# A hybrid decoder layer: key and query chunks loaded later, rotated without a wait on the output product, and split behind the weights on ScalarE

## The reference

```python
q = rotary(q); k = rotary(k) * RET_QK ** -0.5
def step(R, chunk):                       # one chunk of 128 tokens, all heads
    inner = (qc @ kc.T * decay_in) @ vc
    cross = (qc @ R) * xi
    R = R * gamma_c + (kc * zeta).T @ vc
    return R, inner + cross
out = (out - mean) * rsqrt(var + EPS) * g_ret     # over each head's 512 values
y_ret = out * silu(gate_ret)
merged = sigmoid(merge_mla) * (y_mla @ w_proj_mla) + sigmoid(merge_ret) * (y_ret @ w_proj_ret)
x = x + gate * (merged @ w_out);  result = rmsnorm(x, g_final)
```

## Time and profile before

| | us |
|---|---|
| median of 3 runs (1618.77, 1622.36, 1622.16) | 1622.16 |
| the profiled execution's own time | 1618.77 |
| its span, first to last instruction | 1617.0 |
| PE busy in it | 1570.6 (97%) |
| DVE busy | 957.6 (59%) |
| ACT busy | 607.2 (38%) |
| POOL busy | 323.1 (20%) |

### The profile page before, as it was taken

One profiled execution on the slowest core, in us unless ns is written; L12 is line 12 of the kernel. 1 busy time (PEld: TensorE's weight loads), 2 busy tenths in 40 slices (PEclk: granted clock), 3 DMA queues, 4 the chain that ended last, 5 costly groups with the idle time before them and its releaser, 6 DMA issues. The chain is left out here.

```text
span 1617.0 us, 20336 instructions
## 1 busy us (share of the span) xinstructions
PE 1570.6 (97%) x7600; PEld 1310.9 (81%) x7600; DVE 957.6 (59%) x1610; ACT 607.2 (38%) x1057; POOL 323.1 (20%) x280
## 2 busy tenths in 40 slices
PE   5999999999999999999999999999999999999998
PEld 4778888888888888788888878887688888888886
DVE  6984444444444457752565665567987775647544
ACT  5444333333333343342343333334544443213111
POOL 2232223322222200200000000016555530000000
PEclk9999999999999999999999999999999999999999
DMA  9132323323223334799254555548977768335432
GB/s 387 37 130 105 111 111 111 111 106 121 112 104 111 98 93 164 311 410 318 80 199 174 168 195 170 179 137 272 308 237 229 247 205 285 112 131 189 143 104 78
DMA packets 142225, 278.70 MB, mean 172 GB/s; under 512 B 11056, under 2 KB 83632, under 8 KB 133552
## 3 DMA queue, kind: packets, MB, share of 16 engines
q1 hardware_dynamic: 125488, 245.09, 43.6%
q10 hardware_dynamic: 12032, 15.54, 2.9%
q0 software_dynamic: 4608, 16.78, 2.6%
HBM read 182.47 MB, written 94.37 MB: 171 GB/s over the span
## 5 line engine op out<-in xcount | busy, mean ns | idle before, releaser
L1567 DVE TENSOR_TENSOR w_form<-w_pair,w_form 128x512 fp32r<-128x512 f32 x150 | 116.3, 776 | 127.3 <-ACT w_form L1202 125.6
L1202 ACT ACTIVATE w_form<-w_pair 128x512 fp32r<-128x512 f32 x150 | 94.6, 632 | 245.3 <-PE p_banks L2072 237.2
L2069 PE MATMUL p_banks<-h_hi,w_form 128*128 128x512 f32 x300 | 116.8, 389 | 1.1 <-DVE w_form L1567 1.1
L2071 PE MATMUL p_banks<-h_lo,w_form 128*128 128x512 f32 x300 | 116.7, 389 | 0.0
L2072 PE MATMUL p_banks<-h_hi,w_form 128*128 128x512 f32 x300 | 116.7, 389 | 0.0
L1271 ACT ACTIVATE prob<-p_banks,neg_max 128x128 f32<-128x128 f32 (+3 forms) x64 | 47.5, 742 | 181.9 <-DVE neg_max L1675 181.9
L524 ACT ACTIVATE w_hi<-w_raw 128x1024 fp32r<-128x1024 f32 (+2 forms) x69 | 59.5, 865 | 142.2 <-PE p_banks L2319 94.4
L2319 PE MATMUL p_banks<-y_hi,w_lo 128*128 128x512 f32 x256 | 99.6, 389 | 0.0
L1046 POOL DMA_DIRECT2D v_ret<-v_stage x32 | 17.4, 544 | 411.5 <-DVE v_stage L1658 411.5
L2318 PE MATMUL p_banks<-y_lo,w_hi 128*128 128x512 f32 x256 | 99.6, 389 | 0.0
L2317 PE MATMUL p_banks<-y_hi,w_hi 128*128 128x512 f32 x256 | 99.6, 389 | 0.0
(11 more groups left out here) (302 smaller groups left out, 4325.0 us busy)
## 6 DMA issues: line engine op xcount, KB each, us to landing
w_pair<-in_w_pairs SPq DMA_DIRECT2D x25, 1024.0 KB, 4.8
w_raw<-in_w_dense SPq DMA_DIRECT2D x45, 512.0 KB, 4.5
v_ret<-v_stage POOLq DMA_DIRECT2D x32, 512.0 KB, 3.4
v_chunk<-v_ret SPq DMA_DIRECT2D x32, 512.0 KB, 3.6
merge_t<-act_t SPq DMA_DIRECT2D x48, 256.0 KB, 3.5
act_t<-stage SPq DMA_DIRECT2D x40, 256.0 KB, 2.0
act_t<-stage_late SPq DMA_DIRECT2D x40, 256.0 KB, 2.0
ada<-in_w_ada SPq DMA_DIRECT2D x4, 2048.0 KB, 23.7
```

The costliest lines, as they stand in the source:

```text
L1202: self.nc.scalar.activation(self.form[f % FORM_SLOTS][:, 0, :], self.form_source(f), ACT.Copy).then_inc(self.form_hi, 1)
L1567: nc.vector.tensor_tensor(self.form[f % FORM_SLOTS][:, 1, :], self.form_source(f), self.form[f % FORM_SLOTS][:, 0, :].bitcast(F32), ALU.su ...
L2069: self.nc.tensor.matmul(out, w_hi[:, cut], x_hi[:, q, :], start=fresh and q == 0, stop=False, skip_group_check=True)
L2071: self.nc.tensor.matmul(out, w_hi[:, cut], x_lo[:, q, :], start=False, stop=False, skip_group_check=True)
```

## The change

Five edits in the retention loop:

1. SP: the load of query and key chunk n + 4 near the end of step n becomes the load of chunk n + 3 at the top of step n. So each of these loads is issued behind the `yr_done` wait, the `y_ret` store and the gate load of the step before, and ahead of the value chunk.
2. POOL: `rotate_chunk` no longer waits for `out_done`.
3. POOL: the scratch tile changes place at chunk 6 and not at chunk 12, and the last stores of value tiles are issued ahead of chunk 6 and not of chunk 9. The wait for all of these stores moves from chunk 12 to chunk 6.
4. ACT: `high_qk(n + 2)` moves from behind `high_chunk(n + 1)` to the end of step n, behind every split of that step. DVE's order stays.
5. DVE: the 128x1 TENSOR_SCALAR of L1781 (times 1.0, times a column) becomes a 128x1 TENSOR_TENSOR.

```diff
@@ sync_attention
             if g == STEPS + 2:
                 self.load_qk_chunk(sp, 2)
-                self.load_qk_chunk(sp, 3)
                 self.load_set0(sp, 1)
@@ sync_retention
             if n + 3 < CHUNK_STEPS:
+                self.load_qk_chunk(sp, n + 3)
                 self.load_v_chunk(sp, n + 3)
...
-            if n + 4 < CHUNK_STEPS:
-                self.load_qk_chunk(sp, n + 4)
             h, m = divmod(n, NT)
             sp.wait_ge(self.yr_done, n + 1)
@@ gpsimd
         for n in range(2, CHUNK_STEPS):
-            if n == 9:
+            if n == 6:
                 for unit in range(units, FILL_UNITS):
                     self.store_fill(pool, unit)
             self.rotate_chunk(pool, n)
@@ rotate_chunk
-        raw, late = self.qk_raw[n % 3], int(n >= 12)
+        raw, late = self.qk_raw[n % 3], int(n >= 6)
...
-        elif n == 12:
+        elif n == 6:
...
-        if n >= 3:
-            pool.wait_ge(self.out_done, n - 2)
@@ scalar_retention
             if n + 1 < CHUNK_STEPS:
                 self.high_chunk(act, n + 1)
-            if n + 2 < CHUNK_STEPS:
-                self.high_qk(act, n + 2)
             if n == len(FILL_LATE) - 1:
...
                 units += 1
+            if n + 2 < CHUNK_STEPS:
+                self.high_qk(act, n + 2)
@@ vector_retention
-            nc.vector.tensor_scalar(self.ret_rstd[:, cell], self.ret_rstd[:, cell], 1.0, t["ret_cols"][:, col:col + 1],
-                                    ALU.mult, ALU.mult).then_inc(self.stats_done, 1)
+            nc.vector.tensor_tensor(self.ret_rstd[:, cell], self.ret_rstd[:, cell], t["ret_cols"][:, col:col + 1],
+                                    ALU.mult).then_inc(self.stats_done, 1)
```

## The result

The changed kernel takes 1650.3 us (median of 4 runs, 1646.9 to 1652.2); the kernel before took 1621.1 us beside it (4 runs). The ratio is 1.018, with a 95% interval of 1.0158 to 1.0201: 1.8% slower. The forecast was 1640 with a range of 1629 to 1651, so direction and range held and the time came out 10 us above the forecast.

What follows compares the result with a forecast made beforehand. PE was taken to bound nearly everywhere, with DVE setting the pace in early steps. Early 13.9 plus later 5.8 us made 19.7, giving 1638.5 from the profiled execution; with the median 3.4 above that, 1640 us, range 1629 to 1651.

Steps and rivals of the forecast that it cites:

- ACT order: Retention loop: DVE waits in `low_qk` for ACT's splits, then does its own late; early steps 8.6 us, later 5.8.
- stores and scratch: Step 4: chunk 6's rotation waits for the value-tile stores to land, holding up ACT's `high_qk(6)`; 2.5 us taken.
- rotation's overlap: Early steps: rotation released by its load runs beside DVE's `low_qk` and splits; net 2.8 us, bounds 0 to 8.
- 128x1 instruction: DVE statistics: new form taken to cost 0 with one element per partition, bounded to 2.6 us either way.
- Order alone: Retention loop: rotations miss DVE's splits, store wait hidden, only the order costs; 8 to 12 us, 1627 to 1634; chance 0.20.
- The clock falls as well: Steps 3 to 6: pauses of 2 us or more bring PE's clock down, adding 6 to 10 us; 1646 to 1655; chance 0.10.
- signs of being wrong: Loop: `out_n` as early as now despite late `low_qk`, clock down for long, or rotations again in DVE's PSUM part.
- Nothing: Early steps: PE's merge and fill matmuls absorb more than seen; total under 5 us, at 1622; chance 0.07.
- faster: Loop: step 5's overlap (1.9 us) and most of the 7.6 us of waits vanish; 1616 at best; chance 0.06.
- eight meetings: First eight steps: DVE instructions each wait for one rotation instruction, up to 1.3 us; up to 8 us, total near 1645.
- The signs named ahead of the result: Profile after: `out_n` waits 10 us or more, `low_qk` behind ACT some 15, new 1 to 2 us waits in steps 15, 22, 29.

Runs made afterwards that it cites:

- the order alone: Kernel before with only ACT's `high_qk` moved behind the splits of its step, DVE's order unchanged; 1637.0 against 1620.4 us, ratio 1.0103.
- order on ACT and DVE: Kernel before with ACT's `high_qk` and DVE's `low_qk` both moved behind the splits of the step; 1627.5 against 1620.4 us, ratio 1.0043.

## Why the prediction was right in direction and short in size

The last column is what the time falls by when the edit is taken out of the changed kernel.

| term, us | forecast | alone | in the changed kernel |
|---|---|---|---|
| ACT order | 14.4 | 16.6 | 17.4 |
| stores and scratch | 2.5 (0.9 to 3.6) | 5.8 | 10.6 |
| rotation's overlap (edits 1, 2) | 2.8 (0 to 8) | 3.4 | -7.6 |
| 128x1 instruction | 0 (-2.6 to 2.6) | 12.4 | 4.8 |
| sum | 19.7 | 38.2 | (29.2 measured) |

- **ACT order: the mechanism right, one part of its path not.** DVE waits in `low_qk` for ACT's splits and is late with its own, as forecast. The early steps cost 10.9 us in the execution that was profiled (8.6 forecast). But PE was to lose them at `out_n`, and with edit 4 alone these waits stay at 4.3 us in steps 2 to 8: PE stops for `y_lo` in step 7 and for the merge addition in step 8 instead. In the later steps, 15 and 16 cost 5.0 together (1.8 forecast), step 22 1.8 and step 29 0.9 (1.4 each); 11, 18 and 25 cost nothing (0.4 each). The pause in step 15 was near in size, +1.7 us in the changed kernel and +2.2 with edit 4 alone against 1.8. The excess is the clock: in the kernel with edit 4 alone PE's busy time grew by 3.7 us in steps 0 to 7 and by 2.8 in steps 15 and 16, and the term had none of it.
- **Stores: the mechanism right, the term mis-sized.** In the changed kernel the last value tile is ready at 1140.43 and ACT comes to `high_qk(6)` 7.2 us later, as forecast. The rotation ends 14.6 us after the tile and not 10.8, so ACT waits 7.5 us and not 3.6, or the 2.5 that I took. The 3.8 us are in the landing: 6.2 us was the median of this stretch before, and here the first of the two stores landed after 7.1 us and the other, which the rotation waits for, after 10.0 (median 8.5):

```profile
v_ret<-v_stage POOLq DMA_DIRECT2D x2, 512.0 KB, 8.5
```

  What makes it longer is edit 4, not edit 1. The five kernels with the early stores fall into two groups:

| kernel | edit 1 | edit 4 | stores issued against the value chunk's load, us | landing, us | DMA engines busy until then |
|---|---|---|---|---|---|
| stores and scratch alone | no | no | 1.2 ahead | 5.4 | 106% |
| changed, without the order | yes | no | 1.2 ahead | 6.3 | 101% |
| changed | yes | yes | 0.2 behind | 8.5 | 99% |
| changed, without the 128x1 instruction | yes | yes | 0.2 behind | 8.7 | 100% |
| changed, without loads and rotation | no | yes | 0.2 behind | 8.2 | 101% |

  The issues in the last of these, which has no edit 1, POOL and SP:

```profile
1139.80 1.19 POOL L1046 DMA_DIRECT2D v_ret<-v_stage  x2 [12.75 <-DVE v_stage L1658]
...
1139.60 0.33 SPq L827 DMA_DIRECT2D v_chunk<-v_ret  x1
```

  With the order changed, `low_qk` of step 3 is late, so the last value tile and its stores are, and they go out together with the next step's loads of a value chunk, a weight and two MLA outputs. The DMA engines are full in all five, so full engines alone do not tell how long a landing takes. That it is the queueing behind those loads which lengthens it is argued and not shown; no run moves the stores alone. The longer wait then joined with the late `y_lo` and the slow clock: 12.5 us of delay in one step.
- **Overlap: near in size alone, in part by luck, and of the wrong sign in company.** 3.4 us against 2.8. Steps 4 and 7 met the rotation as forecast; steps 1 and 2 did not, steps 3 and 6 did, and step 5 gained 0.7 us and not 1.9. That moving the rotation takes away the clash of edit 5 was not in the sum, since I put that edit at zero.
- **The 128x1 instruction: this is the step that failed.** "With one element in each partition I take 0", and a bound of 2.6 us from the 0.29 us of `inner_lo`. The bound came from an instruction that reads PSUM, and the 0 from the instruction's size; alone the edit cost 12.4 us, and 4.8 in company. The row to take was that of the other two-SBUF-input instructions beside a rotation, 0.68 to 1.28 us: what they lose is not a share of their own length but the rest of POOL's instruction, and a tiny instruction loses as much as a large one. That the rotation of before starts when DVE is at its statistics was in the working. The Trainium skill (SBUF — State Buffer, section "SBUF: two separate sides") says that the two exclude each other for the whole instruction; the trace agrees: 1.23 us beside a rotation instruction of 1.28 us, ending with it, and 0.16 us otherwise. I weighed that rule for the long instructions alone.
- **The range held by luck.** The costs alone add up to 38.2 us, which would have been some 1659 us, outside the range; the change costs 29.2. Edits 1 and 2 shield edit 5, and that they do was not forecast.
- **The rivals.** *Order alone* is out: the store wait was not hidden. (Its terms, 8.6 + 3 to 6 less 1.9, also add up to 9.7 to 12.7 us and not to 8 to 12.) *The clock falls as well* came in part: 13.7 us at a granted clock of 0.51 behind the longest pause, and a short stretch behind step 15; not in each of steps 3 to 6. The clock down for long was one of the signs of being wrong that were named. *Nothing* and *faster* are out. Where the prediction prices eight meetings at up to 1.3 us each, that is up to 10 us and not 8.
- **The signs named ahead of the result.** They came for the new waits in steps 15, 22 and 29 (2.3, 1.2 and 0.7 us), for `low_qk` behind ACT (24.9 us, 18.1 with the order alone, some 15 was said), for the one wait of `high_qk` for POOL, for rotations released by landings and for the unchanged stages behind step 31. They did not for `out_n`: 10 us or more in steps 2 to 8 was said, and those steps have 7.3, since PE stopped for the rotation, the chunk and `y_lo` instead. And `low_qk` at 1.2 us "in many" was 6 of 31 above 1.1 us, with a median of 0.70: with edits 1 and 2 alone it was 14 of 31, and with edit 4 it starts later and meets the rotation less often.
- **Left open.** The 4.8 us of edit 5 in the changed kernel: its instruction is busy for 2.5 us more over the loop (9.3 against 6.8), and the two profiled executions have nearly the same span (1643.7 and 1644.0), so the trace does not show where the rest lies. The one is 4.8 us below its kernel's median and the other 1.6 above, and 4.8 us is hardly more than the uncertainty.

## What to carry to other kernels

Where two engines do the halves of one job from lists in order, their lists must name the jobs in the same order: moving one entry on one engine cost 16.6 us here, and with it moved on both the delay was 0.7 us at the end of the steps in which the lists then agreed. An instruction is not cheap because it is small: look at what it reads and what runs on POOL at that moment, and price a clash at the length of the other engine's instruction. Price a wait on a DMA by landings under the traffic that it will meet (with edit 4, by which the stores are issued some 2 us later, they landed after 8.2 to 8.7 us and not 5.4 to 6.3), and each edit together with the edit that moves its neighbour, since single costs of 38.2 us came to 29.2 together.

## What the hardware showed that was not expected

- A TENSOR_TENSOR of 128x1 with both inputs in SBUF took 0.16 us alone and up to 1.28 us beside POOL's TENSOR_TENSOR of 128x512, while a TENSOR_SCALAR that reads the same column as its scalar stayed at 0.212 to 0.217 us in all 32 steps, in 29 of them with the same rotation beside it.
- Two stores of 512 KB each landed after 5.4 and 6.3 us in two kernels, where they went out 1.2 us ahead of the next load, and after 8.2 to 8.7 us in three, where they went out 0.2 us behind it, with the DMA engines full in all five.
- The length of PE's pause does not say by itself whether the granted clock falls: behind 2.33 us (changed kernel) and 2.89 us (order on ACT alone) it was 0.50, behind 2.86 us at the same place (order on ACT and DVE) it stayed at 1.00.
